# Products of the unit matrix in three of TensorE's early waits, in a decoder step of latent attention, retention and a convolutional feed-forward

## The reference, cut to what matters

```python
xp = layer_norm(concatenate([meta, x_prompt]), ln0_g, ln0_b); xs = layer_norm(x_sample, ln0_g, ln0_b)
h = x @ w_in            # q and kv latents, rope key, retention q / k / v / gate, two branch gates
A = latent attention (prompt: causal; sample: over the paged cache)
B = retention (4 heads, chunks of 128), group norm, swish gate
x = LN1(alpha*x + (sigmoid(g_a) * A @ w_attn_out + sigmoid(g_b) * B @ w_ret_out) @ w_o)
x = LN2(alpha*x + (gelu(causal_dwconv3(x @ W_a)) * (x @ W_g)) @ w_ffn_out)
```

## Time and profile before

| | |
|---|---|
| median of 3 executions | 1014.45 us (1013.73 to 1018.99) |
| span of the profiled execution | 1027.7 us |
| TensorE matmul, busy | 974.2 us (95%) |
| VectorE, busy | 666.5 us (65%) |
| ScalarE, busy | 387.2 us (38%) |
| mean granted TensorE clock | 0.983 |

### The profile page before, as it was taken

How to read it: one execution, slowest core, us unless ns; L and a number is a source line. 1 busy time by engine, 2 the same in 40 slices (tenths; PEclk the granted TensorE clock), 3 DMA queues, 4 the chain that set the end, 5 groups by cost and what they waited for, 6 DMA issues and landing times.

```text
span 1027.7 us, 22122 instructions
## 1 busy us (share of the span) xinstructions
PE 974.2 (95%) x9086; PEld 898.9 (87%) x9086; DVE 666.5 (65%) x1054; ACT 387.2 (38%) x857; POOL 39.1 (4%) x44
## 2 busy tenths in 40 slices
PE   4899999999999999599999999999999999999995
PEld 3899999988888897455569999999999999999995
DVE  7467556765555555888837658697774335767567
ACT  4234332324151514333323323556661124565331
POOL 0000000000000011333100000000000000000000
PEclk9899999999999999899999999999999999999998
DMA  9504444313233324999643934224323243341643
GB/s 256 169 24 106 122 122 108 89 23 102 50 96 85 105 102 158 383 344 354 243 161 118 281 85 125 82 82 115 90 82 93 81 114 83 94 111 56 190 119 124
DMA packets 174772, 136.88 MB, mean 133 GB/s; under 512 B 18707, under 2 KB 162936, under 8 KB 170328
## 3 DMA queue, kind: packets, MB, share of 16 engines
q1 hardware_dynamic: 166442, 93.47, 32.5%
q0 software_dynamic: 5760, 37.75, 9.8%
q10 hardware_dynamic: 2502, 4.68, 1.2%
HBM read 124.18 MB, written 11.80 MB: 132 GB/s over the span
## 4 chain that ended last, share of the span: by engine, by line
PE 78%; DVE 12%; issue 4%; ACT 3%; DMA 1%; ACTq 0%; DVEq 0%; another core or an unknown queue 0%; POOL 0%; POOLq 0%
PE PS L2014 34%; PE PS L2242 8%; PE PS L2694 8%; PE PS L2756 6%; PE PS L2025 3%; PE PS L2471 3%; DVE w_lo L1225 2%; PE PS L2589 2%; PE PS L2414 2%; ACT p_sample L972 2%; PE PS L2279 1%; PE PS L2268 1%; PE PS L2340 1%; DVE y_tok L1734 1%; PE PS L2256 1%
## 5 line engine op out<-in xcount | busy, mean ns | idle before, releaser
L2014 PE MATMUL PS<-x_hi,w_hi 128*128 128x262 f32 (+1 forms) x744 | 164.0, 292 | 2.7 <-DVE x_lo L1272 1.4
L1225 DVE TENSOR_TENSOR w_lo<-w_raw,w_hi 128x2048 fp32r<-128x2048 f32 (+3 forms) x65 | 125.9, 1937 | 59.7 <-ACT w_hi L703 48.2
L2014 PE MATMUL PS<-x_lo,w_hi 128*128 128x262 f32 (+1 forms) x744 | 160.0, 287 | 0.0
L2014 PE MATMUL PS<-x_hi,w_lo 128*128 128x262 f32 (+1 forms) x744 | 159.6, 286 | 0.0
L703 ACT ACTIVATE w_hi<-w_raw 128x2048 fp32r<-128x2048 f32 (+3 forms) x59 | 94.5, 1601 | 145.9 <-PE PS L2014 88.3
L2014 PEld LDWEIGHTS PS<-x_hi,w_hi 128*128 128x128 f32 x744 | 120.7, 190 | 6.0 <-issue 2.4
L2014 PEld LDWEIGHTS PS<-x_lo,w_hi 128*128 128x128 f32 x744 | 120.1, 190 | 0.0
L2014 PEld LDWEIGHTS PS<-x_hi,w_lo 128*128 128x128 f32 x744 | 120.0, 190 | 0.0
L2242 PE MATMUL PS<-x_hi,w_hi 128*128 128x262 f32 (+1 forms) x256 | 78.7, 307 | 0.0
L2242 PE MATMUL PS<-x_hi,w_lo 128*128 128x262 f32 (+1 forms) x256 | 73.3, 286 | 0.0
L2242 PE MATMUL PS<-x_lo,w_hi 128*128 128x262 f32 (+1 forms) x256 | 73.3, 286 | 0.0
(11 more groups left out here) (376 smaller groups left out, 2293.2 us busy)
## 6 DMA issues: line engine op xcount, KB each, us to landing
w_raw<-in_w_ffn_in_dram SPq DMA_DIRECT2D x44, 512.0 KB, 4.5
w_raw<-in_w_in_dram SPq DMA_DIRECT2D x37, 512.0 KB, 6.7
w_raw<-in_w_ffn_out_dram SPq DMA_DIRECT2D x28, 320.0 KB, 3.8
w_raw<-in_w_o_dram SPq DMA_DIRECT2D x12, 512.0 KB, 5.2
w_raw<-in_w_ffn_out_dram SPq DMA_DIRECT2D x16, 384.0 KB, 3.9
gate_scratch<-gate_out ACTq DMA_DIRECT2D x8, 524.0 KB, 2.9
gates<-gate_scratch SPq DMA_DIRECT2D x8, 524.0 KB, 9.0
x_T_scratch<-x_sum_T SPq DMA_DIRECT2D x1, 2144.0 KB, 7.5
```

Of the source, the lines that this page charges most:

```text
L1225: V.tensor_tensor(WL[:, at_, ks], RAW[:, at_, ks], WH[:, at_, ks].bitcast(F32), ALU.subtract).then_inc(s_wsplit, 1)
L2014: last = T.matmul(PS[:, bank, 0:n], w[:, par, kw + k, m * P:(m + 1) * P], x[:, k0 + k, half * n:(half + 1) * n], start=start and k == 0 an ...
```

## The change

A function `keep_warm(n)` is added to TensorE's program. It makes n products of the unit matrix by itself (128 x 128, 32-bit float), all into columns 384 to 511 of PSUM bank 3, which nothing reads. It is called in three places: with 7 products after `x_forward(2)`, ahead of the wait for the first `x_hi`; with 5 ahead of `x_forward(3)`; and with 4 after the second group of 12 products, ahead of the small transposes. No semaphore is added or moved, and no other engine's program is touched.

```diff
+            def keep_warm(n):
+                for _ in range(n):
+                    T.matmul(PS[:, 3, 3 * P:4 * P], IDENT, IDENT, start=True, stop=True, skip_group_check=True)
             for t in range(3):
                 x_forward(t)
+            keep_warm(7)
 ...
                 pe.wait_ge(S["x_feat"], 1)
                 pe.wait_ge(S["x_feat_dve"], 2)
+                keep_warm(5)
                 x_forward(3)
                 tile(0, 1, 8, XH, XL, 0, 1, halves=(0,), ks=range(4))
                 x_forward(4)
                 tile(0, 1, 8, XH, XL, 0, 1, halves=(0,), ks=range(4, 8))
+                keep_warm(4)
                 pe.wait_ge(c2.sem, c2.after(8))
```

## The result

| | before | after |
|---|---|---|
| median of 20 executions | 1018.95 us (1013.73 to 1025.80) | 1022.67 us (1019.49 to 1026.81) |
| span of the profiled execution | 1027.7 us | 1020.6 us |
| instructions | 22122 | 22186 |

The change made the kernel slower by 0.37%: the ratio is 1.0037, with a 95% interval of 1.0023 to 1.0051. The prediction was 1012.7 us, a gain of 0.17% on the three executions shown then. Of the 10 us between 1012.7 and 1022.67, 4.5 are only that the kernel before, timed with more executions, has a median of 1018.95; the other 5.5 are a gain of 1.8 that turned into a loss of 3.7.

A forecast was written before the change was run, and what follows sets the result against it. The prediction took TensorE, with its clock halved after early waits, to bound the kernel. Of 1.76 + 1.80 = 3.56 us it took the middle, 1.78: 1014.45 - 1.78 = 1012.7 us, range 1009.3 to 1016.0.

The forecast's parts named there:

- Bound and target: TensorE bounds most of the kernel; its clock halves after waits of 3.4, 2.0 and 1.4 us, two stretches on the path.
- the "0.9" of the last paragraph: Forecast sign in the profile after: TensorE's 2.0 us wait ahead of tile 3 cut to some 0.9 us.
- What the clock gives back: Full rate in the two stretches on the path, from 26.26 and 35.64 us, saves 1.76 and 1.80, together 3.56 us.
- so they cost nothing directly: Said of the 7 products after tile 2: 1.54 or 3.15 us of work, covered by the 3.41 us wait.
- the price of the products: Each product takes 0.22 us at full rate, 0.45 at half; all 16 take 3.5 to 7.2 us, mostly inside waits.
- I let the whole 3.56 us reach the end: Behind 43.94 us all engines follow TensorE's order, so the profiled execution's whole saving was taken to reach the end.
- All gain: Rival: all executions gain as the profiled one would, 3.56 us, giving 1010.9 us; chance 0.20.
- one fall stays: Rival: one clock fall, at tile 3 or the small transposes, remains; 0.9 us gained in the median, 1013.6 us; chance 0.17.
- It doesn't do what it says: Rival: the products don't hold the clock, or the rotation or a weight load takes the gain; 1014.4 us; chance 0.12.
- Slower: more falls in the sample attention: Rival: the earlier start makes the clock fall in more sample attention requests, 1.6 us each; 1017.5 us; chance 0.06.

The follow-up runs named there:

- e1_after: The changed kernel unchanged, timed again beside the kernel before: 1028.62 us, ratio 1.0000 (0.9978 to 1.0023).
- e2_after: The changed kernel once more, beside the kernel before on another chip: 1023.39 us, ratio 1.0038 (1.0018 to 1.0058).
- e1_before: The kernel before, unchanged, as a check on the comparison and for a second profile: 1027.64 us, ratio 0.9998 (0.9980 to 1.0015).
- e2_afterpad192: The changed kernel with 192 unused semaphore increments at the start of TensorE's program: 1038.13 us, ratio 1.0189 to the kernel before; 1017.7 us less 20.4 of later start.
- e3_mid48: The changed kernel plus 48 one-column products in TensorE's wait ahead of the sample attention: 1037.81 us, ratio 1.0103 to the kernel before.
- e4_after: The changed kernel again, for its profile beside the kernel before on one chip: 1027.97 us, ratio 0.9996 (0.9973 to 1.0019).
- e4_mid48n: The changed kernel plus 48 products with 32 columns of weights in the wait ahead of the sample attention: 1029.60 us, ratio 1.0002 to the kernel before.
- e5_mid48n: The changed kernel plus 48 products with 32 columns of weights ahead of the sample attention, timed again: 1029.30 us, ratio 1.0013 to the kernel before.
- e2_pad64: The kernel before with 64 unused semaphore increments at the start of TensorE's program, no products: 1023.49 us, ratio 1.0047 (1.0025 to 1.0069).
- e2_pad256: The kernel before with 256 unused semaphore increments at the start of TensorE's program: 1047.58 us, ratio 1.0275; 1017.1 us less 30.5 of later start.
- e3_mid16: The kernel before plus 16 one-column products in the wait ahead of the sample attention, no early products: 1027.81 us, ratio 1.0005 (0.9989 to 1.0021).
- e3_mid64: The kernel before plus 64 one-column products in the wait ahead of the sample attention: 1046.74 us, ratio 1.0190 (1.0166 to 1.0213).
- e4_mid16n: The kernel before plus 16 products with 32 columns of weights in the wait ahead of the sample attention: 1029.93 us, ratio 1.0010 (0.9995 to 1.0026).
- e5_before: The kernel before, unchanged, timed again: 1027.53 us, ratio 0.9999 (0.9974 to 1.0024).
- e2: The group of padded and changed kernels timed on one chip, where the kernel before took 1018.71 us.

## Why the prediction was wrong

**Bound and target: right.** Three falls after three waits, two of them on the path, and the products held the clock in all three in the profiled execution. The standing still ahead of tile 3 was 1.6 us, within the 0.9 and some 0.9 more of the working but not the "0.9" of the last paragraph, and no fall followed. What the small transposes do for the third place stayed undecided: the clock held there with the four products in the shown profile, fell in e1_after and e2_after in spite of them, and held in e1_before without any.

**What the clock gives back: right in that profile, too large for the median.** I forecast 3.56 us and found 3.17: the first 8 transposes took 1.09 us where I had 0.89, and the 24 products 3.23 where I had 2.97. For the median I took half, 1.78. The eight profiles with the 16 full products (after, e1_after, e2_after, e2_afterpad192, e3_mid48, e4_after, e4_mid48n, e5_mid48n) have a mean early part of 30.6 us, and the five of before one of 32.0. With the five others that have no full products (e2_pad64, e2_pad256, e3_mid16, e3_mid64, e4_mid16n) the mean without is 31.5. So the gain is 1.0 to 1.5 us by these means, not far above their scatter, and the single values overlap: 29.85 us without products (e1_before), 31.75 with them (e1_after). The profile that was shown had 33.37 us and one of the two longest early parts, so what I wanted to save was in good part that execution's bad luck.

**The step that failed: "so they cost nothing directly", the price of the products.** "I let the whole 3.56 us reach the end" held for what was saved; the term beside it was missing. Behind the early part all work up to 408.6 us and behind 518 us took the same time to within some 0.1 us, the one fall near 228 us aside. (That fall costs 1.4 us and came in 5 of the 10 profiles without full products and in 1 of the 8 with them; that is too few to call it a gain.) But I priced the products only by TensorE's time and covered them with waits ("so they cost nothing directly"). They also are 64 instructions, and they move all code behind them by a quarter of a 16 KB block. e2_pad64 shows that this alone, with no product and no earlier start, costs a ratio of 1.0047 (1.0025 to 1.0069) on a chip of the faster kind; e2_pad256 and e2_afterpad192 show that a move by a whole block costs nothing beyond the padding's own time. The missing term is 4 to 6 us: e2_pad64 lost 4.8, and the sample attention takes 106.9 to 107.2 us in the three kernels moved by 64 that ran on chips where before took 1019 us, and 101.0 and 102.7 in the two moved by 256. Less 1.0 to 1.5 us of gain it leaves about the 3.7 us that were measured.

All eight profiles of kernels moved by 64 have a stop in the sample attention of 0.97 us or more, as the table counts them; the eleven with a move of 0 or 256 stay at 0.60 or less, and all but e3_mid48 and e5_before at 0.43 or less. Each of the eight has its largest stop at L2480 or L2440, by the changed kernel's lines. There are eleven stops of 0.9 us or more in the eight profiles, and every one ends 1.3 to 1.6 us after a packet of code has come in: 485.11 after 483.83 us in the shown profile, 487.60 and 500.73 after 486.20 and 499.19 in e2_after, 487.90 and 501.58 after 486.43 and 500.02 in e2_pad64. Packets come 4 to 10 us apart there, so chance would not do this eleven times.

The Trainium skill, "Runtime: NRT & Kernel Launch", section "Instruction fetch mechanics", says that an engine's program is streamed in blocks of 16 KiB, 256 instructions, over a DMA queue of the engine's own, and that the cost of crossing a block is mostly hidden. The traces agree with the block (51 packets in 0.84 MB). With the hiding they disagree at one place: where the gathers hold 89% of the DMA engines and TensorE has many short instructions, it stood still for 2.13 us, and how much depends on where the blocks lie.

**Why the loss is there on some chips only.** Where before takes 1028 us, a request of the sample attention takes 13.2 us with or without stops, and the ratios are 1.0000 and 0.9996 for the changed kernel. Where before takes 1019 us, it takes 11.9 us without them.

**The rivals.** "All gain" and "one fall stays" fell with the sign. "It doesn't do what it says" is false of the clock. "Slower: more falls in the sample attention" named the right stage and nearly the right loss (3.0 us against 3.7), but the wrong mechanism: e2_after lost its time at a clock of 1.00.

**What stays open.** That a block of code comes late because the gathers fill the DMA engines is argued from three things that the traces show: a packet of code at the same distance ahead of the end of each stop, no semaphore that ends it, and the cure by a shift of 256 instructions. No run slowed or sped up the fetching by itself. For the kernel before unmoved there is no profile from a chip where it takes 1019 us; that its sample attention takes some 102 us there is inferred from its median and from the kernels moved by 256, which also start 20 to 30 us later than it does. That the later start alone takes the stops away is made unlikely by e3_mid48, e3_mid64, e4_mid48n and e5_mid48n: they are moved by 256 without it, and the large stops are gone, though on chips where no time could be won by that. Other moves, by 128 instructions say, weren't tried. What sets the 13.2 us of the other chips wasn't tried. No version that beats the kernel before was found: e2_afterpad192, less its padding, would be 1 us better than before with an interval of more than 3 us to each side.

## What to carry to other kernels

Work put into a wait costs no time of its engine and still costs instructions: ask where the code behind it comes to lie, and test the edit against the same number of empty instructions at the start of the program, which parts the two effects in one run as long as they fit into the first wait (64 did, 256 did not). A stop that ends on "issue", at a place where many short instructions meet full DMA queues, is the sign. A stall of the clock that is read from one execution should be looked for in a second one before it is priced, since these falls come and go between executions of the same program.

## What the runs showed of the hardware

- TensorE's clock falls at other places from one execution to the next: the same early part of the same program took 29.85, 31.78, 31.81, 33.37 and 33.38 us, with falls at different places.
- A product of one column with 128 x 128 weights took 0.11 us for each of its instructions at a clock of 1.00 and 0.21 us at 0.50 (e3_mid64), as much as one of 128 columns (0.11 us in the changed kernel); with 32 columns of weights, in four groups of columns in turn, an instruction of 128 columns took 0.04 us (e4_mid48n).
- An increment of a semaphore by TensorE itself took 0.16 us: 192 of them ended at 30.73 us and 256 at 40.76 us.
- Chips differ by 1% on this kernel (1018.71 to 1029.04 us for the same program), and the traces put it into the stage that gathers cache pages: 101 to 103 us (e2_pad256, e2_afterpad192) against 109 and more in the five profiles of the kernel before.
- 64 added instructions far away moved a stage by 4 to 6 us on the chip of e2, and by too little to measure on the others.
- TensorE's eleven longest stops on "issue" in the sample attention of the kernels moved by 64 ended 1.3 to 1.6 us after a packet of 16 KB of code had come in.
